# Prompt attention in half steps: V held in the array, outputs turned back, three row buffers for q and k

## The reference

```
DILATIONS = ((128, 1), (512, 4), (2048, 16))           # window, dilation
for window, dil in DILATIONS:
    # residue classes mod dil are sub-sequences, in blocks of 128 queries
    scores = q_block @ [previous block, own block of k].T * 64 ** -0.5
    valid  = (dist >= 0) & (dist <= 128) & (key exists)
    lse    = logsumexp(scores);  p = exp(scores - lse)
    o      = p @ [previous block, own block of v]
w = softmax(stack(lses));  out = sum over the patterns of w * o
```

## Time and profile before

| | us |
|---|---|
| median of three runs | 3142.62 |
| the profiled execution | 3147.27 |
| its span, from first to last instruction | 3145.6 |
| prompt attention in it (first issue of a load to the last store's issue) | 637.8 to 1137.1 |

### The profile page before, as it was taken

How to read it: one execution, slowest core, us unless ns; L and a number is a source line. 1 busy time by engine, 2 the same in 40 slices (tenths; PEclk the granted TensorE clock), 3 DMA queues, 4 the chain that set the end, 5 groups by cost and what they waited for, 6 DMA issues and landing times. The chain is left out here.

```text
span 3145.6 us, 42678 instructions
## 1 busy us (share of the span) xinstructions
PE 2880.0 (92%) x16445; PEld 2392.7 (76%) x16445; DVE 1356.0 (43%) x2910; ACT 994.0 (32%) x2044; POOL 414.8 (13%) x556
## 2 busy tenths in 40 slices
PE   5899987967889879599959999999999999999998
PEld 3678876756778867488748888888888888999986
DVE  6446774534455533688623332333223332333321
ACT  3122212245455533466522221222212221223210
POOL 1126874400000000000000000000010000100001
PEclk8999998987889979799979999999999999999999
DMA  7653336543333366566475553555436545454421
GB/s 264 212 175 113 124 111 210 175 133 116 99 98 109 101 263 243 191 203 202 141 229 159 174 177 124 169 186 162 154 127 201 160 148 190 153 157 135 149 83 51
DMA packets 335624, 500.83 MB, mean 159 GB/s; under 512 B 23817, under 2 KB 230921, under 8 KB 326730
## 3 DMA queue, kind: packets, MB, share of 16 engines
q1 hardware_dynamic: 316384, 372.41, 36.9%
q0 software_dynamic: 18672, 125.85, 11.4%
q10 hardware_dynamic: 394, 0.16, 0.0%
HBM read 409.06 MB, written 155.95 MB: 180 GB/s over the span
## 5 line engine op out<-in xcount | busy, mean ns | idle before, releaser
L2210 PE MATMUL f_ps_f<-f_h_f,f_ws_f 128*128 128x512 f32 (+1 forms) x5280 | 1002.6, 352 | 26.9 <-DVE f_ws_f L2270 26.9
L2210 PEld LDWEIGHTS f_ps_f<-f_h_f,f_ws_f 128*128 128x128 f32 x5280 | 859.9, 188 | 169.0 <-DVE f_ws_f L2270 27.0
L2228 PE MATMUL f_ps_f<-f_ws_f,f_aT_f 128*128 128x512 f32 x2244 | 519.2, 393 | 1.0 <-DVE f_tmp_f L2280 1.0
L2228 PEld LDWEIGHTS f_ps_f<-f_ws_f,f_aT_f 128*128 128x128 f32 x2244 | 422.0, 188 | 97.5 <-DVE f_tmp_f L2280 1.5
L2270 DVE TENSOR_TENSOR f_ws_f<-f_raw_f,f_ws_f 128x1024 fp32r<-128x1024 f32 x264 | 315.9, 1224 | 416.7 <-ACT f_ws_f L2242 416.7
L2242 ACT ACTIVATE f_ws_f<-f_raw_f 128x1024 fp32r<-128x1024 f32 x264 | 268.5, 1049 | 421.0 <-PE f_ps_f L2228 394.7
L779 PE MATMUL p_out_ps<-p_w,p_hT 128*128 128x512 f32 x1632 | 386.9, 396 | 6.0 <-DVE p_qk L1027 3.7
L779 PEld LDWEIGHTS p_out_ps<-p_w,p_hT 128*128 128x128 f32 x1632 | 306.3, 190 | 79.9 <-issue 14.1
L2293 DVE TENSOR_TENSOR f_tmp_f<-f_sl_f,f_ps_f 128x512 f32<-128x512 f32 (+1 forms) x110 | 64.6, 588 | 562.1 <-PE f_ps_f L2210 561.6
L344 PE MATMUL a_o_ps<-a_v,a_probsT 128*128 128x64 f32 x1200 | 177.6, 305 | 75.0 <-DVE a_probsT L399 74.9
L344 PEld LDWEIGHTS a_o_ps<-a_v,a_probsT 128*128 128x128 f32 x1200 | 163.2, 216 | 92.1 <-DVE a_probsT L399 82.9
(11 more groups left out here) (316 smaller groups left out, 2753.8 us busy)
## 6 DMA issues: line engine op xcount, KB each, us to landing
f_raw_f<-in_w_gate_dram SPq DMA_DIRECT2D x88, 512.0 KB, 4.1
f_raw_f<-in_w_up_dram SPq DMA_DIRECT2D x88, 512.0 KB, 5.1
f_raw_f<-in_w_down_dram SPq DMA_DIRECT2D x88, 512.0 KB, 3.8
out_dram<-in_cache_k_dram POOLq DMA_DIRECT2D x8, 4088.0 KB, 14.4
out_dram<-in_cache_v_dram POOLq DMA_DIRECT2D x8, 4088.0 KB, 14.5
p_ring<-in_w_ada_dram SPq DMA_DIRECT2D x32, 512.0 KB, 4.8
b_k<-in_cache_k_dram SPq DMA_DIRECT2D x16, 1024.0 KB
b_v<-in_cache_v_dram SPq DMA_DIRECT2D x16, 1024.0 KB
```

The source lines that it names most:

```text
L2210: mm = pe.matmul(out, ws[:, p % SPLIT, a, k * 128:(k + 1) * 128], h2[:, y, k, c0:c1], start=(k == 0 and x == 0), stop=(k == KT - 1 and x = ...
L2228: mm = pe.matmul(ps[down_bank(b, h, j)][:, :], aT[:, a, k, at:at + 128], ws[:, p % SPLIT, y, (k % 2) * 512:(k % 2 + 1) * 512], start=(k == ...
```

## The change

It rewrites `attention_stage`:

- The work goes by half steps i = 0 to 95 (four heads each), written out without hardware loops. In round i PE does: turn k of the next step (even i) or q of the step after that (odd i); `scores(i)`; in odd rounds `back` for step (i-5)/2; `probs(i-2)`; `values(i-3)`.
- There are two banks for everything that is turned (`t_ps[0]`, `t_ps[1]`, taken in turn) and two for the outputs. ACT or DVE copies a turned bank by a fixed rule (`by_act`): k and the first unit of a long half step by ACT, q and the second unit by DVE. In a short step the four heads of a half step are one unit, ACT for the first half and DVE for the second.
- `scores`: kT lies as [pair, slot, key], so that previous and own block are one product of 256 columns where their slots are neighbours; even and odd heads alternate.
- `values`: V (128 x 64) is held in the array and 128 columns of turned probabilities are streamed. Even heads go to partitions 0 to 63 of the bank, odd heads to 64 to 127. The result has channels in its partitions. ACT copies it to `a_oT`, four transposes (`back`) turn it into the same bank, and DVE copies it to `a_o`.
- `a_q` and `a_k` have three buffers, `a_o` four. v is asked for two steps behind q and k.
- The reduction takes the negative scale and the minimum, so L393 and its wait go; the exponential has scale -1. `mix_stage` follows (minimum for maximum, scale -1).

```diff
-        q = P.sb("a_q", [128, 2, AW])
-        k = P.sb("a_k", [128, 2, AW])
+        q = P.sb("a_q", [128, IN, AW])          # IN, V_LATE = 3, 2
+        k = P.sb("a_k", [128, IN, AW])
...
-        o = P.sb("a_o", [128, 2, OROW])
-        t_ps = P.ps("a_t_ps", [128, 512])
+        oT = P.sb("a_oT", [128, 2, PAIRS, QB])
+        o = P.sb("a_o", [128, ORING, OROW])     # ORING = 4
+        t_ps = [P.ps(f"a_t_ps{x}", [128, 512]) for x in range(2)]
...
-            def step(n):
-                p, r = n.slot(2), n.slot(4)
-                wait(sp, kT_ps, n.times(1) - 1)
-                sp.dma_start(q[:, p].unsqueeze(1), rows(t["q"], n)).then_inc(qk_loaded[p], 16)
-                sp.dma_start(k[:, p].unsqueeze(1), rows(t["k_prompt"], n)).then_inc(qk_loaded[p], 16)
-                wait(sp, pv_done, n.times(4) - 8)
-                sp.dma_start(v[:, r].unsqueeze(1), rows(t["v_prompt"], n)).then_inc(v_loaded[r], 16)
+            for n in range(STEPS + V_LATE):
+                p, m = n % IN, n - V_LATE
+                if n < STEPS:
+                    if n >= IN:
+                        wait_turned(sp, ("q", n - IN))
+                    sp.dma_start(q[:, p].unsqueeze(1), rows(t["q"], n)).then_inc(q_loaded[p], 16)
+                    if n >= IN:
+                        wait_turned(sp, ("k", n - IN))
+                    sp.dma_start(k[:, p].unsqueeze(1), rows(t["k_prompt"], n)).then_inc(k_loaded[p], 16)
+                if m >= 0:
+                    if m >= 4:
+                        sp.wait_ge(valued, 2 * (m - 3) + 2)
+                    sp.dma_start(v[:, m % 4].unsqueeze(1), rows(t["v_prompt"], m)).then_inc(v_loaded[m % 4], 16)
...
+            def scores(i):
+                ...
+                        if not has_prev(n):
+                            spans = ((0, n % 4, 1),)
+                        elif n % 4:
+                            spans = ((0, n % 4 - 1, 2),)
+                        else:
+                            spans = ((0, 3, 1), (QB, 0, 1))
+                        for col, slot, w in spans:
+                            mm = pe.matmul(bank[:, at + col:at + col + w * QB], qT[half, n % 3, pair, :],
+                                           kT[half, pair, slot:slot + w, :].rearrange("p a n -> p (a n)"), start=True, stop=True)
...
-                        mm = pe.matmul(o_ps[:, hd * HD:(hd + 1) * HD], prT[:, pair % 2, x, prev * QB:(prev + 1) * QB],
-                                       v[:, (n + -prev).add % 4, hd * HD:(hd + 1) * HD], start=(prev == 0), stop=(prev == last))
+                            mm = pe.matmul(o_ps[n % 2][e * HD:(e + 1) * HD, pair * QB:(pair + 1) * QB],
+                                           v[:, (n - (blocks - 1 - b)) % 4, hd * HD:(hd + 1) * HD],
+                                           prT[:, i % 2, x, c * QB:(c + 1) * QB], start=(b == 0), stop=(b == blocks - 1))
...
+            def back(n):
+                pe.wait_ge(oT_sb, n + 1)
+                for j in range(PAIRS):
+                    mm = pe.transpose(o_ps[n % 2][:, j * 128:(j + 1) * 128], oT[:, n % 2, j, :], ident[:, :])
+                mm.then_inc(oT_back, 1)
...
+            for i in range(HALVES + 4):
+                n, quad = divmod(i, 2)
+                u = ("q", n + 2) if quad else ("k", n + 1)
+                if u[1] < STEPS:
+                    turn_rows(u)
+                if i < HALVES:
+                    scores(i)
+                if quad == 1 and i >= 5:
+                    back((i - 5) // 2)
+                if 0 <= i - 2 < HALVES:
+                    probs(i - 2)
+                if 0 <= i - 3 < HALVES:
+                    values(i - 3)
...
-                mx.then_inc(masked, 1)
-                dve.wait_ge(masked, n.times(2) + quad + 1)
-                dve.tensor_scalar(nb[:, p, 4 * quad:4 * quad + 4], o[:, p, AW + 4 * quad:AW + 4 * quad + 4], -SCALE, None,
-                                  ALU.mult).then_inc(negmax, 1)
```

More of the change, by code:

```diff
@@ new lines, in oT_out @@
+            def oT_out(n):
+                act.wait_ge(valued, 2 * n + 2)
+                if n >= 2:
+                    act.wait_ge(oT_back, n - 1)
+                act.activation(oT[:, n % 2].rearrange("p j n -> p (j n)"), o_ps[n % 2][:, :], ACT.Copy).then_inc(oT_sb, 1)
+            turned_out(act, move, ("k", 0))
+            for i in range(HALVES + 4):
+                n, quad = divmod(i, 2)
+                if quad == 0 and n + 1 < STEPS:
+                    turned_out(act, move, ("k", n + 1))
+                if 0 <= i - 1 < HALVES:
+                    exps(i - 1)
+                if 0 <= i - 2 < HALVES:
+                    for u in units(i - 2):
+                        if by_act(u):
+                            turned_out(act, move, u)
+                if quad == 0 and i >= 4:
+                    oT_out((i - 4) // 2)
@@ L369, in _, with move @@
         @block.vector
         def _(dve):
[L371 to L385 removed]
+            def move(dst, src):
+                return dve.tensor_copy(dst, src)
@@ L386, in maxima @@
+            def maxima(i):
+                n, quad = divmod(i, 2)
+                prev = has_prev(n)
+                w = 2 * QB if prev else QB
+                dve.wait_ge(scored, i + 1)
+                if i >= 4:
+                    wait_turned(dve, units(i - 4)[-1])
+                if quad == 0 and n >= ORING:
+                    dve.wait_ge(o_stored[n % 2], 16 * ((n - ORING) // 2 + 1))
+                dve.memset(gate[:, quad:quad + 1], 0.0)
                 for j in range(4):
@@ L403, in outputs_out @@
-            def outputs_out(n):
-                dve.wait_ge(pv_done, n.times(4) + 4)
-                dve.tensor_copy(o[:, n.slot(2), 0:AW], o_ps[:, :]).then_inc(o_sb, 1)
-            def step(n):
-                first, last = n.i is None and n.add == 0, n.i is None and n.add == STEPS - 1
-                if not last:
-                    queries_out(n + 1)
-                for quad in range(2):
-                    if not first:
-                        probs_out(n + -1, 2 * quad)
-                    maxima(n, quad)
-                if not first:
-                    outputs_out(n + -1)
@@ L1859, in weigh @@
                     act.wait_ge(gap, n + 1)
[L1860 removed]
+                    act.activation(wt[:, :, :], wt[:, :, :], ACT.Exp, scale=-1.0).then_inc(expd, 1)
             def x1_squares(n):
```

304 lines of the change are left out of this document (150 added, 154 removed).

## The result

The changed kernel takes 3004.98 us (four runs, 3002.19 to 3009.26) beside 3143.43 us for the kernel before on the same chip (four runs, 3142.11 to 3147.3): ratio 0.9565, interval 0.9552 to 0.9579. It is 138 us faster. The profiled execution takes 3005.6 us, its span 3003.7, so it lies 141.7 us under the profiled execution of before (3147.27).

A forecast was written before the change was run, and what follows sets the result against it. Short steps were bound by the store's latency, long ones by PE's work plus one wait. PE steps of 344.6 us ended the stage 137.7 earlier; less 14 for clock and 9 for waits, gain 115: 3030 us, range 2980 to 3100.

The forecast's parts named there:

- the ideal end of the stage: Changed attention stage: 641.6 + 3.5 start + 344.6 of PE steps + 9 end = 998.7, 137.7 us earlier than before.
- added-up waits: Changed stage: 9 us taken off for slack in even rounds, `back` on ACT's copy, and the end beside big loads.
- Nearly everywhere: DVE's maxima: with four output buffers the 110 us wait for the store of two steps before goes nearly everywhere.
- In a long step the store isn't late: Long steps before: maxima ahead of the copy on DVE, not the store, leave PE idle 1.61 us in one half.
- the halves overlap in `values`: PE's `values`, long half: two column halves work at once, 16 instructions in 0.95 us (0.86 to 1.72) for 1.72.
- The rival without overlap: `values`: column halves don't work at once, costing 61 us; gain 54, time 3089; chance 0.10.
- the other terms of PE: Long half besides `values`: turn 0.44, way in 0.17, scores 1.10, transposes 0.90, ways 0.20 each; step 8.36 with turning back.
- a chain of 9 us: Stage's end: from the last scores to the last copy to `a_o`, maxima through final copy with latencies, 9 us.
- The rival of a clock that stays at 0.80: Short stretch: gaps keep the mean clock at 0.80, 72 us more; gain 43, time 3100; chance 0.12.
- Both are enough for the first of them: New tokens' loads: head start of 29 us, 38 before, suffices for the first load; cost 0 to 5 us.
- One sign of being wrong: Profile after: short steps above 7 us, a clock under 0.85, or later stages of another length would be wrong.
- the third rival: Something slow between engines: late stores, even rounds waiting for ACT, or both with slow shape changes; gain 75, time 3068; chance 0.13.

## Why the prediction was right, and where it was off

**The account.** The prediction forecast 3030 us and a gain of 115 in the profiled execution; it was 141.7. By its own terms: the ideal end of the stage was put at 998.7 and the last copy to `a_o` ends at 978.9, 20 us earlier; 14 us for the clock and 9 for added-up waits were taken off and weren't lost on top of that; 12 us were given back at the next stage's start, priced at 0; and 4 later on, of which nothing was said. 115 + 20 + 23 - 12 - 4 = 142.

**Which part did it.** From the stage's first load to its last store: before 499.2 us, with four output buffers alone 374.5, the new rounds with probabilities held 347.7, the changed kernel 342.2. So 124.7 us come from the buffers, 26.8 from rounds and merged scores, 5.5 from holding V. In times it is 113, 20 and 5 of 138. For a long step at the full clock the runs give the chain 8.87 (old order, four buffers), 8.78 (rounds, scores not merged), 8.54 (merged), 7.98 (V held). The 8.78 is from the three long steps whose scores can't be merged, in the run that holds the probabilities; in the changed kernel the same three are only 0.13 over the others. Merged scores alone weren't run in the old order.

**Right: the store's latency is the bound of short steps, and PE is what is late next.** Short steps went to 5.45, for which the sum said 5.66, and PE is busy for 0.94 of the first window and 0.99 of the third. "Nearly everywhere" was everywhere: no wait for a store is in the list. The stores also land sooner in the new order (2.3 us in the median for 4.4), which the prediction didn't foresee and, with four buffers, didn't need: the kernel before with four buffers has the gain at 3.8 to 3.9 us to landing.

**Wrong: "In a long step the store isn't late".** The prediction counted two losses in two kinds of step and gave the 1.61 us of the long step to the order of maxima and copy. The kernel before with four buffers has that order and not that loss. The step that failed was to take the releaser of one row ([3.98 <-PE a_p_ps L331], which I had left out of the rows) at its word where a store issued 4.5 us before was the other candidate (it landed 0.1 us before DVE went on), and where the maxima's own input had long been there. The total wasn't harmed, since the change mends both; what each part is worth was, and my expectation of 3087 us for that run shows it (3030).

**Right, and the largest term: the halves overlap in `values`.** I took 0.95 for 16 loads with ends 0.86 and 1.72; it is 0.85. The rival without overlap falls, and the run with one half after the other shows what the order of the instructions does to it. (That rival's price has a slip: 0.47 for a short half should be 8 x 0.107 - 0.48 = 0.38, which makes 58 us of the 61.) The Trainium skill, on the page TensorE: Matmul & The Clock Gate (The mechanism), says that a load of weights overlaps with matmuls in flight only when the row group differs. Here both halves use all rows and differ in their columns, and 16 loads take 0.85 where 16 x 0.107 one by one would be 1.72. Taken at its word for column halves the sentence doesn't hold here, and the measurement decides. With the Trainium skill's page TensorEngine Tiling (Array Packing) (Key Properties), by which different tiles load and multiply in parallel, the trace agrees.

**Mis-sized, each by a little: the other terms of PE.** Turning with its way in took 0.59 (0.61), scores with the way out 1.06 (1.10), transposes with the way in 1.02 to 1.08 (1.10), values with the way out 1.02 to 1.17 (1.15), `back` 0.38 (0.44). The step is 7.98 for 8.36. The Trainium skill's rule that a change of mode drains the engine (TensorEngine Tiling (Array Packing), Key Properties) agrees in kind, since each of the four changes has its row, at 0.17 us, in places 0.33; it doesn't cost enough to eat the gain. Over 24 long steps at 0.38, three at 0.25 and 21 short ones at 0.21 that makes 14 of the 20 us by which the stage beat its ideal. Of the other 6, 1.7 were there before PE's first transpose, which starts at 639.9 for the 641.6 of before. The rest lies in the start and end, where I had added a chain of 9 us on top of all the steps though the last rounds overlap with it: the last four stores come 22 us after the one before them, less than three steps.

**Off: the clock.** I took 0.96 for the stage; the rows show 0.94 for dilation 16 (1.00 from 660 us on) and 1.00 from there to the end, 0.98 in all. The rival of a clock that stays at 0.80 falls. With the stalls gone, it rose in the kernel before with four buffers too (0.96 from 637 to 1020 us), so the old clock of the earlier trace rows was a consequence of the store's wait and part of its price. The run without late v is the same thing in the other direction: stalls of 4 us and a clock of 0.81.

**Mis-sized: the loads for the new tokens.** "Both are enough for the first of them" looked at the loads themselves. What came late was what stands beside and behind them: the stage's last store (6.3 us to landing for 2.8), for which the barrier waits, and one small load in their queue (13.0 us for 1.8). The prediction had the row of a store late beside big loads (7.27) and used it for the steps, not for the store that ends the stage. The head start of 38 us had covered both, 18 us didn't; I had put it at 29, from seven rounds at the old pace. Measured 12 us for 0 to 5, and the run with the loads spread gives 10 of it back.

**The signs it named.** The paces of 5.45 and 7.98 us and the 0.85 us of `values` are each a little under what the profile after was said to show (5.7 to 6, 8.4 to 8.8, 0.9 to 1.0), and the clock is as said. One sign of being wrong did come: what lies behind the stage has another length than before, by the 12 us at its start and 4 later on.

**Not decided here.** That even rounds wait for ACT was a part of the third rival; PE's longest wait for ACT in the list is that of `back`, 7.3 us in all, and the next 4.8. The 2.3 us lost between the next stage and the feed-forward part have no cause that I could name.

## What to carry to other kernels

Before an order of work is rewritten, give the buffer that is stored two slots more and measure: here it was four fifths of the gain in a handful of edited lines. Where a wait names several semaphores, list every one that ended within a few tenths of a microsecond of the release, a DMA's landing among them, before believing the named one. And where a stage becomes faster, follow the queue behind it: requests that had 38 us of cover have 18, and the last store beside them and the small load behind them are what is late. A latency belongs to the order that it was measured in: the same store took 4.8 us to land in the old order and 2.6 in the new one.

## What the runs showed of the hardware

- Loads of weights into the two column halves of the array (128 x 64, float32, 128 columns streamed) go on at once if they alternate: 16 in 0.85 us, 8 in 0.42 with runs of two or four to one half. With runs of eight, 16 take 1.34; while one half works alone its loads start 0.11 us apart. Into the whole array 16 take 1.86, 0.11 apart too (all at the full clock).
- A change between whole array, row halves and column halves shows as 0.17 us of "issue" before PE's loads at the full clock, 0.33 in places.
- A store of 264 KB landed after 4.8 us in the median where it was issued right behind three loads of 256 KB (the kernel before, 695 to 735 us), after 2.6 where it was issued ahead of them (three output buffers, the same stretch), and after 6.3 beside 14 MB of large loads.
- A load of 64 KB issued behind 14 MB of large ones in the same queue landed after 13.0 us; with those loads spread over twelve steps, PE used it 1.8 us after its issue.
- Behind the barrier the next stage's first instruction came 4.87 to 4.91 us after the last store had landed, in all twelve kernels.
